# Two of six chunks of value and gate rows made in the joint ahead of a mixer

## The reference

```python
v = p[..., M_W:2 * M_W]                                  # M_W = 512
ig = p[..., g0:g0 + 2 * M_HEADS] + i_bias                # g0 = 1536, M_HEADS = 4
fg = p[..., g0 + 2 * M_HEADS:M_COLS] + f_bias
```

## Time and profile before

| what | us |
|---|---|
| median of 3 runs | 2297.11 |
| fastest and slowest run | 2296.42, 2307.28 |
| profiled execution: span | 2300.2 |
| profiled execution: own device time | not listed apart from the runs above |
| TensorE busy in the span | 2226.9 |
| mean granted TensorE clock | 0.986 |
| first work of `stage_ffn_1_2` | 626.3 |
| joint ahead of the second mixer, from its 15 idle products to the border | 1530.5 to 1546.8 |
| value and gate rows of the second mixer | 1549.5 to 1607.0 |
| the rest of the mixer's inputs | 1607.0 to 1692.2 |

### The profile page before, as it was taken

How to read it: one execution, slowest core, us unless ns; L and a number is a source line. 1 busy time by engine, 2 the same in 40 slices (tenths; PEclk the granted TensorE clock), 3 DMA queues, 4 the chain that set the end, 5 groups by cost and what they waited for, 6 DMA issues and landing times. The chain is left out here.

```text
span 2300.2 us, 26544 instructions
## 1 busy us (share of the span) xinstructions
PE 2226.9 (97%) x10359; PEld 1740.7 (76%) x10359; DVE 1108.0 (48%) x2054; ACT 492.7 (21%) x1144; POOL 695.8 (30%) x549
## 2 busy tenths in 40 slices
PE   6998989999999999999999999999999999999998
PEld 4443677777677888888888888885557588888887
DVE  5858965655428842345655325441614341112454
ACT  3102332333422000101300011130324440010012
POOL 0000000000104656654465656500000105555642
PEclk8999999999999999999999999999999999999999
DMA  9624345544412462224154412330112122322230
GB/s 346 220 93 125 98 146 183 161 141 122 146 54 93 164 200 75 76 76 124 60 191 153 145 53 76 87 109 24 50 42 74 37 74 74 102 81 62 76 101 37
DMA packets 255639, 250.20 MB, mean 109 GB/s; under 512 B 20098, under 2 KB 207772, under 8 KB 255388
## 3 DMA queue, kind: packets, MB, share of 16 engines
q1 hardware_dynamic: 255080, 248.37, 34.2%
q10 hardware_dynamic: 436, 0.15, 0.0%
HBM read 243.25 MB, written 4.19 MB: 108 GB/s over the span
## 5 line engine op out<-in xcount | busy, mean ns | idle before, releaser
L2167 POOL TENSOR_TENSOR w_sums<-ring 128x512 f32<-128x512 f32 x66 | 90.9, 1378 | 493.2 <-POOLq L1464 301.5
L2195 POOL TENSOR_TENSOR hidden<-rstd,h_act 128x256 f32<-128x256 f32 x66 | 53.5, 811 | 355.2 <-DVE h_act L2371 355.2
L2371 DVE TENSOR_TENSOR h_act<-ps,rstd 128x256 f32<-128x256 f32 x78 | 33.0, 424 | 224.7 <-PE ps L2069 128.1
L2051 PE MATMUL ps<-h_sums,w_sums 128*128 128x256 f32 x528 | 127.4, 382 | 1.2 <-DVE h_sums L2307 0.7
L2063 PE MATMUL ps<-h_sums,w_sums 128*128 128x256 f32 x528 | 125.0, 380 | 2.4 <-DVE rstd L2341 2.4
L2074 PE MATMUL ps<-h_act,w_sums 128*128 128x256 f32 x528 | 124.8, 380 | 1.4 <-DVE h_act L2335 1.4
L2069 PE MATMUL ps<-h_sums,ring 128*128 128x256 f32 x528 | 124.9, 380 | 1.2 <-DVE rstd L2348 1.2
L2017 PE MATMUL ps<-h_act,ring 128*128 128x256 f32 x528 | 125.4, 382 | 0.1
L2057 PE MATMUL ps<-h_act,ring 128*128 128x256 f32 x528 | 124.7, 379 | 0.0
L2025 PE MATMUL ps<-h_act,ring 128*128 128x256 f32 x528 | 124.3, 380 | 0.0
L2341 DVE TENSOR_TENSOR rstd<-ps,h_act 128x256 f32<-128x256 f32 x78 | 33.1, 424 | 182.0 <-PE ps L2051 159.9
(11 more groups left out here) (479 smaller groups left out, 4468.4 us busy)
## 6 DMA issues: line engine op xcount, KB each, us to landing
ring<-in_ffn_w_in SPq DMA_DIRECT2D x66, 1024.0 KB, 7.6
ring<-in_w_mod SPq DMA_DIRECT2D x12, 2048.0 KB, 7.9
ring<-in_w_gate_up SPq DMA_DIRECT2D x22, 1024.0 KB, 7.7
ring<-in_ffn_w_out SPq DMA_DIRECT2D x32, 704.0 KB, 6.1
mod_half<-in_w_ada SPq DMA_DIRECT2D x16, 1024.0 KB, 8.5
ring<-in_w_in SPq DMA_DIRECT2D x6, 2048.0 KB, 8.1
ring<-in_ffn_w_out SPq DMA_DIRECT2D x8, 1408.0 KB, 7.1
ring<-in_w_down SPq DMA_DIRECT2D x16, 704.0 KB, 6.2
```

What stands on the lines that cost most here:

```text
L2051: last = pe.matmul(pb, s2[:, k], F.t2[:, k], start=(k == 0), stop=(k == 3))
L2167: pool.tensor_tensor(s1, a21, a22, ALU.add).then_inc(S["wsum"].sem, 1)
L2195: pool.tensor_tensor(one[:, j], F.gate1[f % 2], F.got21[f % 2], ALU.mult)
```

## The change

The value and gate products of one chunk become a function, `value_rows`, and the banks they go to another, `value_banks`. In the joint, TensorE now makes chunk 0 of the context where the 15 idle products stood, does the sums of x's second half, and then makes chunk 1, followed by 20 idle products instead of 38. The mixer makes chunks 2 to 5 alone. The gate weights are loaded at the beginning of `stage_ffn_1_2`, into a part of the constants that only the first mixer uses; their semaphore and that of the rows are shared by both stages. The turns of the gate rows now lag two chunks behind the products. VectorE's code copies all six chunks in the mixer as before, from other banks for chunks 0 and 1.

```diff
--- before.py
+++ after.py
@@ -287,6 +287,8 @@
         K.pool = Steps(nc.alloc_semaphore("pool_step"))
         K.sem = nc.alloc_semaphore
         K.sb = sb
+        K.gate_w = K.cst[:, CONST["rot"][0]:CONST["rot"][1]].rearrange("p (k n) -> p k n", k=KT)
+        K.gates_in, K.row_mm = nc.alloc_semaphore("gates_in"), nc.alloc_semaphore("row_mm")
         K.mod_sum, K.mod_mm = nc.alloc_semaphore("mod_sum"), nc.alloc_semaphore("mod_mm")
         K.mods_summed = K.mods_turned = 0
         K.norm_sems = {n: Tally(nc.alloc_semaphore(f"norm_{n}")) for n in ("sq", "mm", "std", "tmp")}
@@ -2385,6 +2387,23 @@
         spare(2)
 
 
+def value_rows(K, pe, c, values, gates):
+
+    w = K.ring.take(pe, "v").rearrange("p (k n) -> p k n", k=KT)
+    for k in range(KT):
+        x = (K.x if c < CC else K.h)[:, k, c * P:c * P + P]
+        pe.matmul(values, x, w[:, k, :], start=(k == 0), stop=(k == KT - 1))
+        last = pe.matmul(gates, x, K.gate_w[:, k, :], start=(k == 0), stop=(k == KT - 1))
+    last.then_inc(K.row_mm, 1)
+
+
+def value_banks(K, c):
+
+    if c < CC:
+        return K.ps[c][:, :], K.ps[2][:, 16 * c:16 * c + 16]
+    return K.ps[4 + c % 2][:, :], K.ps[6 + c % 2][:, 0:16]
+
+
 def stage_ffn_1_2(K, out):
     N = K.norm_sems
     with ExitStack() as st:
@@ -2400,10 +2419,15 @@
                 fast_tensor(K, F0, pe)
                 fast_tail_tensor(K, F0, pe)
                 fast_tensor(K, F1, pe)
-                fast_tail_tensor(K, F1, pe)
+                x_sum(K, F1.T, pe, 0, 0)
+                y_sum(K, F1.T, pe, 1)
+                x_sum(K, F1.T, pe, 0, 1)
+                pe.wait_ge(K.gates_in, 16)
+                value_rows(K, pe, 0, *value_banks(K, 0))
                 x_sum(K, F1.T, pe, 1, 0)
                 x_sum(K, F1.T, pe, 1, 1)
-                idle_products(K, pe, 2, 38)
+                value_rows(K, pe, 1, *value_banks(K, 1))
+                idle_products(K, pe, 3, 20)
 
             @block.scalar
             def _(act):
@@ -2429,7 +2453,9 @@
 
             @block.sync
             def _(sp):
-                K.ring.load_ahead(sp)
+                gates = K.A["w_in_2"][0].rearrange("(k p) n -> p k n", p=P)[:, :, M_G:M_POOL]
+                sp.dma_start(K.gate_w[:, :, :], gates).then_inc(K.gates_in, 16)
+                K.ring.load_ahead(sp, "o")
 
 
 DIRS = {0: list(range(CH)), 1: [c for c in range(CC)][::-1] + [c for c in range(CC, CH)][::-1]}
@@ -2452,7 +2478,6 @@
         with ExitStack() as st2:
             M.gr = K.sb("gate_rows", [P, CH, 16], st2)
             M.u = K.sb("mu_t", [P, MH, TOK], st2)
-            M.gw = K.sb("gate_w", [P, KT, 16], st2)
             mix_inputs(K, M, st2)
         mlstm(K, M)
 
@@ -2460,8 +2485,9 @@
 def mix_inputs(K, M, st):
 
     nc, A = K.nc, K.A
-    w_in, rmm, rk, tr, g0, a1, chunks, tb = (K.sem(f"mi_{n}") for n in (
-        "w_in", "row_mm", "row_kept", "turn", "gate_rows", "gate_act", "gate_chunks", "back"))
+    rk, tr, g0, a1, chunks, tb = (K.sem(f"mi_{n}") for n in (
+        "row_kept", "turn", "gate_rows", "gate_act", "gate_chunks", "back"))
+    w_in, rmm = K.gates_in, K.row_mm
     tile_mm, tile_kept, cv, sl, qm, qk, q_in = (K.sem(f"mi_{n}") for n in (
         "tile_mm", "tile_kept", "conv", "silu", "qk_mm", "qk_kept", "q_in"))
     bias = K.sb("g_bias", [MH, 2, 2], st)
@@ -2488,19 +2514,13 @@
                                         const(K, "ident"))
                 last.then_inc(tr, 1)
 
-            w = K.ring.take(pe, "v").rearrange("p (k n) -> p k n", k=KT)
-            pe.wait_ge(w_in, 48)
-            for c in range(CH):
-                if c >= 2:
+            for c in range(CC, CH):
+                if c >= CC + 2:
                     pe.wait_ge(rk, c - 1)
-                for k in range(KT):
-                    x = (K.x if c < CC else K.h)[:, k, c * P:c * P + P]
-                    pe.matmul(K.ps[4 + c % 2][:, :], x, w[:, k, :], start=(k == 0), stop=(k == KT - 1))
-                    last = pe.matmul(K.ps[6 + c % 2][:, 0:16], x, M.gw[:, k, :], start=(k == 0), stop=(k == KT - 1))
-                last.then_inc(rmm, 1)
-                if c:
-                    turn(c - 1)
+                value_rows(K, pe, c, *value_banks(K, c))
+                turn(c - 2)
             K.ring.left(rmm, CH)
+            turn(CH - 2)
             turn(CH - 1)
 
             w = K.ring.take(pe, "u").rearrange("p (k n) -> p k n", k=KT)
@@ -2616,8 +2636,9 @@
 
             for c in range(CH):
                 dve.wait_ge(rmm, c + 1)
-                dve.tensor_copy(M.gr[:, c, :], K.ps[6 + c % 2][:, 0:16])
-                dve.tensor_copy(M.v[:, c, :, 0:P], K.ps[4 + c % 2][:, :].rearrange("p (h v) -> p h v", h=MH)).then_inc(rk, 1)
+                values, gates = value_banks(K, c)
+                dve.tensor_copy(M.gr[:, c, :], gates)
+                dve.tensor_copy(M.v[:, c, :, 0:P], values.rearrange("p (h v) -> p h v", h=MH)).then_inc(rk, 1)
                 if c:
                     gate_row(c - 1)
             gate_row(CH - 1)
@@ -2671,7 +2692,6 @@
 
         @block.sync
         def _(sp):
-            sp.dma_start(M.gw[:, :, :], A["w_in_2"][0].rearrange("(k p) n -> p k n", p=P)[:, :, M_G:M_POOL]).then_inc(w_in, 16)
             for i, src in enumerate((A["i_bias_2"], A["f_bias_2"])):
                 sp.dma_start(bias[:, i, :], src[0].rearrange("d h -> h d"),
                              allow_slow_non_contiguous=True).then_inc(w_in, 16)
```

## The result

The median of 9 runs of the changed kernel is 2287.61 us (2286.18 to 2293.9), that of 9 runs of the kernel before 2302.43 us (2296.42 to 2311.03). The ratio is 0.9947, with a 95% interval of 0.9932 to 0.9962: 12.2 us faster, between 8.7 and 15.7. The forecast was 2285.1 us in a range of 2281.5 to 2289.5, and -0.52%.

The account below looks back on a forecast made before the run. TensorE's own line of work, busy 97% of the span, was taken as the bound. Joint +8.9, two chunks -17.1, low clock -1.8, border -2.5, first turn -0.4, rows' end +1.0: 12.0 us earlier, 2285.1 us (-0.52%), range 2281.5 to 2289.5.

Parts of the forecast that it names:

- The joint: Last joint, with chunks 0 and 1 in place of idle products: TensorE's work there ends 8.9 us later.
- The border: Between joint and mixer: no load waited for, so TensorE's gap shrinks from 2.78 to 0.30 us; at most 0.94.
- The clock behind the wait: First two chunks of the mixer: low clock after the DMA wait cost about 1.8 us, which goes.
- The end of the rows: From the turn behind chunk 5 to "u": turns lagging two chunks add 1.04 us, bounds 0.7 to 1.5.
- The sum: All terms up to the first product of "u": it starts 12.0 us earlier, at 1595.05 instead of 1607.03.
- How the numbers follow: Chances from a half-per-cent limit (11.5 us): faster 0.48, within 0.49, slower 0.03; the forecast's own case 0.55.
- the dear border: Joint-to-mixer border costs 0.94 us, or tenths are lost at each new seam: 2285.7 to 2286.5; chance 0.10.
- rival 3: Further on, clock falls shift with the work's timing: two fewer give 2281.5, as many more 2288.7; more gained, chance 0.09.
- Everything behind 'u' keeps its distance: After the rows: later work moves along unchanged, with 30 us of slack covering the gate arithmetic.
- rival 1: End of the rows: two close idle stretches bring a new clock fall costing 1.8 us, giving 2286.9; chance 0.18.
- Rival 4: Joint, 1530.5 to 1555.6: half-narrow products fail to hold the clock, 25 us more, 2310; chance 0.03.
- Rival 5: Joint and mixer: the joint's added time equals the mixer's saving, nothing changes; nothing or only half gained, chance 0.05.

Follow-up runs that it names:

- load_only: Kernel before with only the gate-weight load moved to the feed-forward stage, all six chunks left in the mixer: joint to "u" 72.52 us against 76.54, ratio 0.9978 to 1.0004.
- no_idle: Changed kernel without the 20 idle products at the joint's end: joint to "u" 60.33 us against 64.86, ratio to the kernel before 0.9952.
- one_row_no_idle: Changed kernel with only chunk 0 in the joint, turns one behind, no idle products at its end: joint to "u" 67.75 us, median 2296.53 us.
- before_again: The kernel before, unedited, profiled and timed again: joint to "u" 76.71 us against 76.54, ratio 1.0011 (0.9993 to 1.0028).

## Why the prediction was right, and where it was not

**The reading of the bound** held. In all edited versions J moved by what the edit adds to or takes from TensorE's line, and by the falls of the clock.

**The joint**: 8.9 us later forecast, 9.1 measured. From the start of J to the end of the idle products it is 1550.97 - 1525.58 = 25.39, against 25.15 in the working: 0.2 us short, since the sums took 3.54 instead of 3.46 and the idle products 4.71 instead of 4.55 to their modelled end. The cover for ScalarE was as worked out.

**The border**: 0.30 taken, 0.30 measured. The end of 0.94 was wrong: in that row ScalarE was the last to finish, and TensorE's idleness contained the wait for it.

**The clock behind the wait**: 1.8 us forecast to go; load_only gives 1.7 beside 2.3 us of wait. The changed kernel has 1.00 over all of its rows in all four profiles.

**The end of the rows**: +1.04 forecast, 3.51 - 2.48 = +1.03 measured, in idle stretches of 1.01 and 0.86.

**The sum**: -12.0 forecast for the path up to "u", -11.7 measured: the joint +9.1, two chunks -17.1, their low clock -1.8, the border -2.5, the first turn -0.4, the end of the rows +1.0.

**The step that failed** is the one from the sum to the chances ("How the numbers follow"). The sum said that 12 us, 0.52%, are gained, and the step made of it that no change beyond half a per cent was the likeliest outcome, 0.49 against 0.48. It rested on "half a per cent is about what a measurement of this kernel can tell from no change". What the runs showed in its place: with 9 runs each the ratio was 0.9947 with an interval of 0.15% to each side (0.9932 to 0.9962), and the kernel before against itself, with 12 and 26 runs, came out at 1.0011 with 0.18%. The limit of what can be told was a third of what the step took, and all four intervals of the changed kernel lie below 1. The prediction had the numbers for this: by its own prices the new fall (2286.9) and the dear border (up to 2286.5) are gains of 10 us and more too. With the forecast's own case and rival 3 that makes 0.92 for a gain of at least 10 us, where the step counted those two cases, and three tenths of the forecast's own, as no change that can be told. Its own words carried half of the doubt: "the forecast is just past it".

On which side of half a per cent the effect lies is not known even now: 0.48% by all runs, 0.50% set by set, and the ratios were 0.9947, 0.9967, 0.9945 and 0.9943. That some loss could come out never had support in the rows, and the 0.03 for it was ample.

**A second step failed**, at a smaller price: "Everything behind 'u' keeps its distance". It doesn't always: the fall of the clock 72 us behind "u" costs 1.7 us in two of four profiles. The prediction had allowed for falls further on in either direction (rival 3), but gave a chance, 0.09, only to fewer of them; and it had looked for one at the end of the rows (rival 1), which appeared in no_idle only. That takes the mean effect from 11.7 to about 11.

**Luck.** That the first ratio, -0.53%, agrees with the forecast of -0.52% to a hundredth of a per cent is luck: J gave 0.3 us less than forecast, and one of the later ratios was -0.33%. That the first median lies in the range is in part luck too. The range was tied to a "before" of 2297.11, while over all runs the mean of the kernel before is 2301.3; the medians of the three repeats, 2291.96, 2289.94 and 2290.38, and the mean over all runs, 2290.3, lie above its end of 2289.5.

Of rival 4, that products of which every second pass is narrow don't hold the clock, nothing is left: 26 us of them and of sums ran at 1.00 in the joint. Rival 5 is out by J.

## What to carry to other kernels

Products that only fill time are a map of where real work can go: find work whose inputs are ready, put it there, and check which chain of the other engines needed the cover, since one chunk without the second left TensorE idle for 6 us. After such a move look at the idle products that remain; the last 20 had become pure length. And when the gain looked for is under a per cent, measure it by a stretch between two marks inside the profile: J repeated to 0.2 us, where the runs spread over 15. Then compare what lies behind the second mark too, since one_row_no_idle lost 4.1 us there and load_only 1.8.

## What the runs showed of the hardware

The granted clock fell to its lower level in places where TensorE was not idle at all: behind products of four rows, 72 us behind "u", in some executions and not in others of the same kernel, with 1.5 to 1.7 us lost each time. Behind idleness of 2.78 and 2.95 us at the mixer's start it fell in both profiles of the kernel before, and behind 0.30 to 0.45 us in none of the other versions; 6.07 and 9.64 us of idleness came with longer falls; and behind stretches of 1.01 and 0.86 us close together it fell in one profile (no_idle) out of five that had them. The fall in before_again:

```profile
1547.00:1548.00 1.00, 1.00 (x4) 0.56 (x3) 0.00 (x0) 0.00 (x0) 0.00 (x0) 0.50 0.00 0
```

The Trainium skill, "TensorE: Matmul & The Clock Gate", section "HAM oscillation — how this bites in real kernels", tells of falls behind waits for DMA that are longer than the one here. The trace of the kernel before agrees in kind, with a shorter wait, 2.78 us, and 0.50 behind it. The falls behind busy stretches of small products are another case.

The first mixer of the same instructions took from 620.7 to 630.3 us in these profiles, 9.6 of the 15 us over which the single runs spread; the longest runs, of 2310 us, were not profiled. Its cause is open: the clock differs there (0.85 against 0.94 over one stretch of the same work), but whether it is what differs first was not tried.
